# Two transformer blocks on one core: forget-gate rows by DMA, filter taps in two halves of the array's rows, operands at other addresses, first context units and MLP entries respaced

## The reference

```python
# forgetting attention: logits + (c[q] - c[k]), c the running sum of the log gates
c = jnp.cumsum(log_f, axis=-1)
s = q @ k.T * scale + (c[..., q, None] - c[..., None, k])

# implicit filter, 256 positions x 2048 columns (forward | backward offsets), normalized by column
h = jnp.sin(freq * (z @ w1 + b1))
h = jnp.sin(freq * (h @ w2 + b2))
h = h @ w3                                # w3: 64 x 2048
filt = h * (jnp.exp(-t * deltas) + FILTER_SHIFT)
kern = kern * rsqrt(sum(kern * kern, axis=0))

# HGRN2: projections of context and latent tokens, then per head a scan over chunks
p_lat = u_lat @ w_in;  p_ctx = u_ctx @ w_in

x = x + rmsnorm(mix @ w_out, g_post)      # mix: the 32 heads' outputs
y = square(relu(h2 @ w_up)) @ w_down      # MLP, 2048 -> 8192 -> 2048
```

## Time and profile before

| | |
|---|---|
| median of 3 runs | 2637.64 us (2637.2 to 2637.88) |
| profiled execution | 2638.05 us |
| its span | 2635.8 us |
| mean granted TensorE clock | 0.999 of full speed |
| PE busy | 2613.5 us, 99% |
| DVE, ACT, POOL busy | 1860.2, 1333.2, 283.0 us |
| HBM read over the span | 565.78 MB, 216 GB/s |

### The profile page before, as it was taken

How to read it: one execution, slowest core, us unless ns; L and a number is a source line. 1 busy time by engine, 2 the same in 40 slices (tenths; PEclk the granted TensorE clock), 3 DMA queues, 4 the chain that set the end, 5 groups by cost and what they waited for, 6 DMA issues and landing times.

```text
span 2635.8 us, 42187 instructions
## 1 busy us (share of the span) xinstructions
PE 2613.5 (99%) x17844; PEld 2375.3 (90%) x17844; DVE 1860.2 (71%) x2237; ACT 1333.2 (51%) x1785; POOL 283.0 (11%) x257
## 2 busy tenths in 40 slices
PE   9999999999999999999999999999999999999998
PEld 9888976998998988988999899999898898998997
DVE  5555665899999777787678967677656675446555
ACT  5455553554444444466774346666454444443444
POOL 1332321010000000000010211120000000000011
PEclk9999999999999999999999999999999999999999
DMA  9645454668687787876666735446667786555653
GB/s 320 181 144 160 146 175 151 208 246 304 253 289 286 280 315 287 298 264 213 168 216 240 270 121 160 144 145 209 208 204 248 253 301 208 190 181 192 189 192 128
DMA packets 287339, 572.30 MB, mean 217 GB/s; under 512 B 9846, under 2 KB 29073, under 8 KB 286704
## 3 DMA queue, kind: packets, MB, share of 16 engines
q1 hardware_dynamic: 281456, 548.69, 61.1%
q0 software_dynamic: 5696, 20.92, 2.8%
HBM read 565.78 MB, written 3.27 MB: 216 GB/s over the span
## 4 chain that ended last, share of the span: by engine, by line
PE 96%; DVE 2%; ACT 1%; issue 0%; POOL 0%; ACTq 0%; DVEq 0%; POOLq 0%
PE p_gemm L2232 51%; PE p_gemm L2297 32%; PE p_gemm L2258 3%; PE p_gemm L2310 1%; PE p_b L2492 1%; PE p_b L2523 1%; DVE w_lo L1271 1%; PE p_b L2692 1%; PE p_b L2701 1%; PE p_b L2586 1%; PE p_b L2343 0%; PE p_gemm L2251 0%; PE p_b L2506 0%; ACT w_hi L707 0%; PE p_b L2750 0%
## 5 line engine op out<-in xcount | busy, mean ns | idle before, releaser
L1271 DVE TENSOR_TENSOR w_lo<-w_raw,w_hi 128x1024 fp32r<-128x1024 f32 (+1 forms) x864 | 1064.6, 1236 | 659.1 <-ACT w_hi L707 657.3
L707 ACT ACTIVATE w_hi<-w_raw 128x1024 fp32r<-128x1024 f32 (+1 forms) x864 | 897.2, 1041 | 1168.0 <-PE p_gemm L2232 664.6
L2232 PE MATMUL p_gemm<-h_hi,w_hi 128*128 128x256 f32 x2904 | 823.7, 284 | 1.9 <-DVE w_lo L1271 1.9
L2232 PE MATMUL p_gemm<-h_lo,w_hi 128*128 128x256 f32 x2904 | 816.0, 281 | 0.0
L2232 PE MATMUL p_gemm<-h_hi,w_lo 128*128 128x256 f32 x2904 | 815.9, 281 | 0.0
L2232 PEld LDWEIGHTS p_gemm<-h_hi,w_hi 128*128 128x128 f32 x2904 | 547.2, 188 | 10.9 <-issue 5.7
L2232 PEld LDWEIGHTS p_gemm<-h_lo,w_hi 128*128 128x128 f32 x2904 | 547.4, 189 | 0.9
L2232 PEld LDWEIGHTS p_gemm<-h_hi,w_lo 128*128 128x128 f32 x2904 | 547.3, 188 | 0.0
L2297 PE MATMUL p_gemm<-w_hi,a_hi 128*128 128x512 f32 x1008 | 393.2, 390 | 0.0
L2297 PE MATMUL p_gemm<-w_hi,a_lo 128*128 128x512 f32 x1008 | 392.4, 389 | 0.0
L2297 PE MATMUL p_gemm<-w_lo,a_hi 128*128 128x512 f32 x1008 | 392.3, 389 | 0.0
(11 more groups left out here) (440 smaller groups left out, 2522.5 us busy)
## 6 DMA issues: line engine op xcount, KB each, us to landing
w_raw<-in_w_mlp SPq DMA_DIRECT2D x128, 1024.0 KB, 5.2
w_raw<-in_w_in SPq DMA_DIRECT2D x107, 1024.0 KB, 5.3
ada_w<-in_w_ada SPq DMA_DIRECT2D x96, 1024.0 KB, 6.2
w_raw<-in_w_up SPq DMA_DIRECT2D x64, 1024.0 KB, 8.8
w_raw<-in_w_down SPq DMA_DIRECT2D x64, 1024.0 KB, 9.4
w_raw<-in_w_out SPq DMA_DIRECT2D x32, 1024.0 KB, 5.1
w_raw<-in_w_in SPq DMA_DIRECT2D x36, 768.0 KB, 5.2
cmp_w<-in_phi_w POOLq DMA_DIRECT2D x2, 2048.0 KB, 14.7
```

The source lines that it names most:

```text
L707: act.activation(WH[:, s % 4, :, 0:n], RAW[:, s // 2, 2 * (s % 2):2 * (s % 2) + 2, 0:n], ACT.Copy)\
L1271: dve.tensor_tensor(WL[:, s % 4, :, 0:n], RAW[:, s // 2, 2 * (s % 2):2 * (s % 2) + 2, 0:n], WH[:, s % 4, :, 0:n].bitcast(F32), ALU.subtrac ...
L2232: ins = pe.matmul(dst, w[:, s % 4, kk, cols], x[:, k, :], start=k == 0 and m % 2 == 0 and i == 0, stop=k == KC - 1 and i == 2, skip_group_ ...
```

## The change

1. The four `fox_row` steps of PE are gone. POOL stores the gate rows in DRAM before head unit 2 and reads them back, spread over 128 partitions, into `fox_rows` before unit 4; `fox_bias` reads those. ACT's first copy of mixed heads, into the same place, waits for `fox_bias`.
2. The filter's second layer gives its 64 rows twice, `flt_w3` lies as 128 rows x 1024, and the two matmuls of a tap group read rows 0 to 63 and 64 to 127. DVE adds the two halves of the squares, and the norm matmuls are 8 in place of 16 per group.
3. The mixed heads after the first four are in `mix_hi`, `mix_lo` (at 96 K and 112 K, 0 modulo 256) in place of `h_hi`, `h_lo`; latent tokens in `l_hi`, `l_lo`, 32 bytes below where `a_hi`, `a_lo` were (224 modulo 256). The scan's small tiles that shared that region move by the same 32 bytes.
4. The eight updates of the residual stream go two to a unit over four units, in place of 3, 3 and 2, and what follows stands a unit later; context heads are turned after unit 6 of a block, in place of 5.
5. In both MLPs' first unit the third turn stands between the high and the low part. Before the first MLP the update pieces come in the order of the turns.

```diff
-U_SCALE = (6, 11, 19, 33)
+U_SCALE = (7, 11, 19, 33)
...
+        XH = at("mix_hi", 96 * K, [P, KC, T], F32R)
+        XL = at("mix_lo", 112 * K, [P, KC, T], F32R)
...
+        L0 = A0 - 32
+        LH = at("l_hi", L0 + 16 * K, [P, KC, T], F32R)
+        LL = at("l_lo", L0 + 32 * K, [P, KC, T], F32R)
...
-        W3 = at("flt_w3", A0 + 20 * K, [FHID, 2 * HGW])
+        W3 = at("flt_w3", A0 + 20 * K, [P, HGW])
...
-        FF = at("hg_f", A0, [P, 2, T])
+        FF = at("hg_f", L0, [P, 2, T])
...
+                if u == 2:
+                    pool.wait_ge(S("fox_sums"), 1)
+                    pool.dma_start(fox_dram[:, :], PJ[32:40, CH["misc"], :]).then_inc(S("fox_row"), 16)
+                if u == 4:
+                    pool.wait_ge(S("fox_row"), 16)
+                    pool.wait_ge(S("tab_stored"), 32)
+                    pool.wait_ge(S("cmp_mm"), 3)
+                    pool.dma_start(FROW[:, :, :], fox_dram[None, :, :].to_broadcast([P, HEADS, T])).then_inc(S("fox_row"), 16)
...
+                if m == 0:
+                    act.wait_ge(S("fox_bias"), 4)
...
-                        if s == 5:
+                        if s == 6:
                             turned_out(h)
...
-                    dve.scalar_tensor_tensor(BX[:, h, 0:P], ps[:, T * i:T * i + P], cq[0], CAUSAL[:, 0:P],
+                    dve.scalar_tensor_tensor(BX[:, h, 0:P], FROW[:, h, 0:P], cq[0], CAUSAL[:, 0:P],
...
-                dve.tensor_tensor(HB[:, dc, :], HB[:, dc, :], WIN[:, dc, :], ALU.add).then_inc(S("flt_ss"), 1)
+                if dc == 0:
+                    dve.tensor_tensor(HB[:, 0, :], HB[:, 0, :], WIN[:, 0, :], ALU.add).then_inc(S("flt_ss"), 1)
+                else:
+                    own(dve.tensor_tensor(HB[:, 1, :], HB[:, 1, :], WIN[:, 1, :], ALU.add))
+                    dve.tensor_tensor(HB[:, 1, :], HB[:, 1, :], HB[:, 0, :], ALU.add).then_inc(S("flt_ss"), 1)
...
-                    if r in (1, 2, 3):
+                    if 1 <= r < 5:
...
-                        for i in range(3 * (r - 1), min(8, 3 * r)):
+                        for i in range(2 * (r - 1), 2 * r):
...
                 for part in range(2):
                     if part == 1:
+                        between(2)
                         pe.wait_ge(S("tok_lo"), tok0 + 1)
...
                 for i in range(2):
-                    col = HGW * i + 512 * hf
-                    ins = pe.matmul(bank(i, "flt_sd", n + 1)[:, :], FA[:, P * dc:P * dc + P], W3[:, col:col + 512], start=True, stop=True)
+                    rows = slice(FHID * i, FHID * i + FHID)
+                    ins = pe.matmul(bank(i, "flt_sd", n + 1)[:, :], FA[rows, P * dc:P * dc + P], W3[rows, 512 * hf:512 * hf + 512],
+                                    start=True, stop=True)
...
-                        for dc in range(2):
-                            ins = pe.matmul(PB[2][:, 4 * hf + cc:4 * hf + cc + 1], HB[:, dc, P * cc:P * cc + P], ONE[:, 0:1],
-                                            start=dc == 0, stop=dc == 1)
+                        ins = pe.matmul(PB[2][:, 4 * hf + cc:4 * hf + cc + 1], HB[:, 1, P * cc:P * cc + P], ONE[:, 0:1],
+                                        start=True, stop=True)
...
-                        gemm_unit(b, None, s, AH, AL)
+                        gemm_unit(b, None, s, LH, LL)
...
-                    if h >= 0 and s == 5:
+                    if h >= 0 and s == 6:
                         turn_heads(h)
```

More of the change, by code:

```diff
@@ L828, in mixed_top @@
                 act.wait_ge(S("att_out"), MIX_DONE[m])
-                act.activation(O0H[:, :, :] if m == 0 else mix_part(HH, m), mix_src(m), ACT.Copy).then_inc(S("wo_hi"), 1)
+                act.activation(O0H[:, :, :] if m == 0 else mix_part(XH, m), mix_src(m), ACT.Copy).then_inc(S("wo_hi"), 1)
             for s in range(SLOTS):
@@ L1502, in fox_bias @@
             def fox_bias(r):
-                dve.wait_ge(S("fox_row"), r + 1)
                 if r == 0:
+                    dve.wait_ge(S("fox_row"), 32)
                     dve.wait_ge(S("misc_nat"), 1)
@@ L1712, in x1_piece, with x1_half @@
                        .then_inc(S("x1_upd"), 1)
-            for j in range(2):
+            def x1_half(j):
                 for tb in range(2):
@@ L1718, in _ @@
                        .then_inc(S("x1_upd"), 1)
-            x1_piece(1)
+            for j in range(3):
+                x1_half(j)
             for j in range(3):
                 rest_gain(2, j, "g_mlp_pre")
-                if j:
+                if j == 0:
+                    x1_half(3)
+                else:
                     x1_piece(1 + j)
@@ L2466, in misc @@
                 ins.then_inc(S("misc_turned"), 1)
-            def fox_row(r):
-                ps = bank(2 * ((U_DIL + 1 + r) % 2) + 1, "fox_bias", r + 1)
-                for i in range(2):
-                    h = 2 * r + i
-                    ins = pe.matmul(ps[:, T * i:T * i + T], IDN[32:40, 32 + h:33 + h].to_broadcast([8, P]),
-                                    PJ[32:40, CH["misc"], :], start=True, stop=True)
-                ins.then_inc(S("fox_row"), 1)
             def scores(u):
@@ L2544, in _ @@
                     weighted_values(u)
-                if s in FOX_SLOT:
-                    fox_row(FOX_SLOT.index(s))
                 u = unit_at.get(s - D_T)
@@ L2568, in filter_hidden @@
                     pe.wait_ge(S("flt_sin"), 1)
-                    pe.matmul(bank(0, "flt_arg", 2)[0:FHID, 0:T], FW[:, 1, :], FA[:, :], start=True, stop=True).then_inc(S("flt_mm"), 1)
+                    pe.matmul(bank(0, "flt_arg", 2)[:, 0:T], FW[:, 1:3, :].rearrange("p i n -> p (i n)"), FA[0:FHID, :],
+                              start=True, stop=True).then_inc(S("flt_mm"), 1)
             def filter_taps(n):
@@ L2607, in _ @@
             keep_busy(1, 7)
-            for j in range(3):
+            for j in range(2):
                 turn_x1(j)
@@ L2613, in mlp_block @@
                 if ready is not None and s == 0:
-                    first_unit(b, HH, HL, ready[1])
+                    first_unit(b, HH, HL, ready[1], turn_x1 if b == B_MLP1 else turn_u2)
                 elif q < 4:
@@ L2819, in _ @@
             turn_u2(0, (1,))
-            for j in range(1, 3):
-                turn_u2(j)
+            turn_u2(1)
             for g in range(GROUPS):
```

84 lines of the change are left out of this document (43 added, 41 removed).

## The result

| | before | changed |
|---|---|---|
| median | 2637.76 us (4 runs, 2637.2 to 2638.69) | 2624.42 us (4 runs, 2623.78 to 2624.96) |
| ratio | | 0.995, 95% interval 0.9937 to 0.9962 |
| profiled execution, span | 2635.8 us | 2622.9 us |

The change took off 13.3 us, 0.5%. Forecast were 16.2 us and 2621.4 (2616 to 2629). The sign and the range held; 2.9 us of the expected gain are missing, and the interest of this case is where they went.

A forecast was written before the change was run, and what follows sets the result against it. PE, busy 99% of the span at 2.4 GHz, was taken as the bound. Terms -4.2 -0.1 -1.9 -1.7 -1.3 -5.2 -1.8 +0 sum to -16.2 us off the median 2637.64: 2621.4 us, range 2616 to 2629.

The forecast's parts named there:

- Forget-gate rows: Four fox_row steps of 1.06 us leave PE, with POOL's two replacement DMAs covered by its idle time: -4.2 us.
- Taps 0 and 1 and spectrum 0: Filter stretch up to the first spectrum: faster PE meets a new wait of about 2.3 us on DVE, leaving -0.1 us.
- Taps 2 and 3, norms and mixed behind spectrum 0: Later filter work: tap groups on two array halves -1.9, halved norm matmuls -1.7, stationary operand's address -1.3 us, all earned.
- mixed: Mixed heads' stationary operand moved from 224 to 0: 6.5 ns on 288 matmuls, 1.9 us, 0.55 eaten by the wait: -1.3.
- Entries: Starts of both MLPs with the third turn inside the first unit: -0.45 us at the first, +0.44 at the last, together 0.
- Context start: Respaced residual updates -1.8, later head turning -0.95, new waits for ACT's copies in two heads +1.0 us: together -1.8.
- Latent operands: Moving operands of 3072 latent matmuls go from address 0 to 224, 120.0 to 118.3 ns each: -5.2 us.
- the one without a new wait: At spectrum 0 DVE's and ACT's lists shorten with PE, so no wait appears: -2.3 more, 2619.1 us; chance 0.08.
- The address rival: Address does not cause the latent and mixed matmul spacing, so -5.2 and -1.3 vanish: 2627.9 us; chance 0.10.
- The rival that the halves don't run side by side: Filter taps' two array halves are only queued closer; taps 2, 3 give 0: +1.9, 2623.3 us; chance 0.06.
- The rival of the other side: Base 224 slows the latent matmuls by 6.5 ns each, +20.0 in place of -5.2: 2646.6 us; chance 0.02.

The follow-up runs named there:

- combined kernel: Changed kernel with spectrum 0 waiting for sums only and copied ahead of ACT's split, DVE's scan outputs, scores and states earlier, last MLP entry as before: 2618.6 us.
- addr_only: Kernel before with only the address moves of latent operands, mixed heads and the scan's small tiles: 2632.84 us, ratio 0.998.
- latent0: Changed kernel with latent operands and the scan's small tiles back at 0 modulo 256: 2627.67 us, ratio to before 0.9963.
- h0: Changed kernel with h_hi, h_lo moved from 224 to 0 modulo 256: 2637.19 us, ratio to before 0.9997.
- residues: Changed kernel with latent operands at 128, h at 64 and mixed heads at 128 modulo 256: 2620.32 us in 2 runs, ratio to before 0.9935.
- taps_one_half: Changed kernel with both matmuls of a tap group on rows 0 to 63, one after the other: 2626.15 us, ratio to before 0.9953.

## Why the prediction came out as it did

By its own steps, each against the stretch of the trace that holds it:

- **Forget-gate rows**, -4.2: measured -4.27, and +3.8 when undone. The cover on POOL and the DMAs' slack were as said.
- **Taps 0 and 1 and spectrum 0**, -0.1 with a new wait of 2.3: measured -0.16, with waits of 1.19 and 0.73, 1.9 in all. I had the place half right: the first part of the wait already stands before taps 1, whose banks DVE has not read yet. DVE's additional sum is there as forecast:

```profile
408.48 0.69 DVE L1699 TENSOR_TENSOR flt_b<-flt_b 128x512 f32<-128x512 f32 x1
419.09 0.95 PE L2612 MATMUL p_b<-ones,flt_b 128*128 128x1 f32 x8
419.90 0.49 PE L2326 MATMUL p_gemm<-w_hi,mix_hi 128*128 128x512 f32 x1
...
422.86 1.13 PE L2596 MATMUL p_b<-flt_w,flt_a 64*128 64x512 f32 x4
423.91 0.50 PE L2326 MATMUL p_gemm<-w_hi,mix_hi 128*128 128x512 f32 x1
```

- **Taps 2 and 3, norms and mixed behind spectrum 0**, -1.9 -1.7 -1.3 = -4.9: measured -3.99. From start to the next matmul's start, as the forecast counted, a tap group fell from 1.91 to 1.05 (422.86 to 423.91), 0.86 and not 0.95, and the norm groups from 1.70 to 0.81 (419.09 to 419.90), 0.89 and not 0.85. The two kinds give -1.7 and -1.8, 3.5 of the 3.6. The term that was wrong is mixed: it put seven units before spectrum 0, and there are twelve, so that only 144 matmuls stand behind it and not 204, and they gained 5.3 ns each in place of 6.5. The stretches of 24, 48 and 72 went from 5.79, 11.35 and 16.93 to 5.68, 11.12 and 16.51 us: -0.8 in place of -1.3. Spectrum 1 comes 0.2 later after spectrum 0 than before (6.36 and 6.16 us), behind ACT's copies, and itself takes 0.1 longer. The mechanisms were right, and these amounts are what the terms were off by.
- **Entries**: -0.48 and +0.43 against -0.45 and +0.44. The second entry is a loss, and its undoing is part of the combined kernel.
- **Context start**, -1.8: measured -1.80, with some luck. PE's waits there are the ones named, 0.4 for the modulation rows and 0.4 for the first of the two heads' copies on ACT (the second, 0.3, stands in the next stretch). But the 0.95 that turning the heads later was to give did not come: the wait of 0.93 for `hg_ke` is gone, and one of 0.6 for `w_lo`, at 1236, came in its place. The respaced updates alone made the sum: the 240 matmuls among them went from 41.66 to 39.71 us by the starts, -1.95.
- **Latent operands**, -5.2: here the prediction failed. The spacing is what it said (118.3 ns), but -3.52 was earned, and -3.89 in addr_only, without the other parts. The step took the latent stage for bound by PE, because the list of waits had nothing in it for the scan. In fact DVE's list was already holding each head by some 0.36 us, and what PE gains by the address meets DVE's keys, outputs and splits. The question that I put to every other part, whether the feeding engine is early enough, was not put to this one. The combined kernel shows it: the same spacing, another order of DVE's list, and the stage gives 4.2 us more. The seven periods from head to head earned 1.2 us (198.35 to 197.16) of the 2.2 that their matmuls save, so 1.0 of the missing 1.7 is there. Ahead of them stand the second wait for `hg_ken`, 0.3, and one of 0.5 before the first head's outputs (L2769), which the kernel before did not have.
- The remaining 0.9 in the profiled execution is its late start, and belongs to no step.

Of the rivals, the one without a new wait fell with the waits of 1.19 and 0.73. The address rival fell with latent0, h0 and residues: the spacing of 256 columns took the values 117.8, 118.3 and 120.0 ns with no other edit than addresses. The Trainium skill's rule ("TensorE: Matmul & The Clock Gate", "Back-to-back issue gap"), by which the gap goes by the number of columns and the clock alone, is not what these traces show. The rival that the halves don't run side by side fell with 1.05 us for a group, and 1.91 again in taps_one_half. An estimate by what the Trainium skill has for packed matmuls ("TensorE: Matmul & The Clock Gate", "Measured speedup vs the span model") takes 0.95 off a group, where 0.86 was measured. The rival of the other side, latent matmuls slower at 224, fell at 34.09/288 = 118.4 ns. That the total lay in the forecast's range is no proof of the sum: the latent term was 1.7 us too large, the mixed one 0.5, and the context start was right as a sum and not in its parts.

## What to carry to other kernels

Where PE is busy for 99%, a list of waits without entries in a stage does not say that PE bounds the stage with room to spare: before multiplying a saving by its count, look in the timeline of one period of the stage for how long before PE's use each input is ready. A wait that is taken away where one engine's list feeds PE at several places comes back at the next place; take them together, and read the distance from period to period and not the list. Once the order is tight, the base address of PE's operands is worth a look, as an experiment that costs one line: it made 12.8 us here between two places of one pair of arrays.

## What was not expected of the hardware

The spacing of back-to-back matmuls at the same clock depends on the operand's start address, and differently for the two sides. By the address modulo 256: moving side, 256 columns, 120.0 ns at 0, 118.3 at 224, 117.8 at 64, and at 128 between 118.5 and 120.0 by the place in the program. Stationary side with 512 moving columns: 226.7 to 227.1 ns at 0, 233.2 at 224, 233.3 at 64, 232.4 at 128. The addresses are offsets from the kernel's base, which it rounds up to a multiple of 64, so the true remainders may all be shifted by the same amount. That 256 is the period is not shown: two places with remainder 0 (96 K, and where `a` lies) gave the same spacing, and so did two with 224, but no run tried other periods. Whether it is the high part's or the low part's address, or their distance of 16 K to each other and to the weights, stays open.

With `h` at 64, two whole stretches of the first MLP, 16 and 7 units, ran at 113.3 ns a matmul by their starts in the trace, at the same places in both kernels that have it there (in residues from 668 to 712 us and from 875 to 894), and no stretch in the other twelve traces did. What these stretches have in common, and how to get it everywhere, is open. At 4.5 ns for each of some 8700 matmuls, 39 us as an estimate, it would be worth more than the whole change, were it to be had for all.
